# Moving the small PSUM copies of an attention stage from ScalarE to VectorE

## The reference

```python
for l in range(DEPTH):
    h = rms_norm(x, attn_norm[l])
    proj = h @ w_in[l]
    ...
    o_mla = mla_attention(...)      # softmax(q k^T * scale, causal) @ v, 8 heads
    o_nsa = nsa_attention(...)      # gates * (compressed, selected, window), 8 heads
    x = x + jnp.concatenate([o_mla, o_nsa], axis=-1) @ w_out[l]
    h = rms_norm(x, ffn_norm[l])
    x = x + conv_ffn(h, ...)
return rms_norm(x, final_norm)
```

## Time and profile before

| | |
|---|---|
| median of three runs | 1314.37 us |
| the profiled execution, its own time | 1314.45 us |
| its span in the profile | 1312.5 us |
| TensorE matmuls busy | 1272.6 us (97%) |
| VectorE busy | 687.2 us (52%) |
| ScalarE busy | 655.7 us (50%) |
| GpSimd busy | 67.8 us (5%) |
| attention stage of layer 0, of layer 1 | about 102 to 250 us, 749 to 897 us |

### The profile page before, as it was taken

One profiled execution on the slowest core, in us unless ns is written; L12 is line 12 of the kernel. 1 busy time (PEld: TensorE's weight loads), 2 busy tenths in 40 slices (PEclk: granted clock), 3 DMA queues, 4 the chain that ended last, 5 costly groups with the idle time before them and its releaser, 6 DMA issues.

```text
span 1312.5 us, 18515 instructions
## 1 busy us (share of the span) xinstructions
PE 1272.6 (97%) x6630; PEld 1050.4 (80%) x6630; DVE 687.2 (52%) x1194; ACT 655.7 (50%) x1223; POOL 67.8 (5%) x157
## 2 busy tenths in 40 slices
PE   8999999999999999999999999999999999999997
PEld 6997677788888888888889867677888888888886
DVE  5435667355555555533363456772655555554334
ACT  4337789445444444322352468892454544443223
POOL 2013110000000000000010311100000000000000
PEclk9999999999999999999999999999999999999999
DMA  6420101123333333322143210012223333333211
GB/s 205 124 89 1 65 1 46 35 80 105 98 98 98 98 97 100 108 96 97 53 121 94 65 65 1 1 50 84 81 76 96 97 96 97 98 103 118 96 64 64
DMA packets 121003, 107.04 MB, mean 82 GB/s; under 512 B 3764, under 2 KB 110486, under 8 KB 120947
## 3 DMA queue, kind: packets, MB, share of 16 engines
q1 hardware_dynamic: 118912, 101.13, 25.0%
q0 software_dynamic: 1456, 3.52, 0.9%
q10 hardware_dynamic: 578, 1.64, 0.3%
HBM read 104.19 MB, written 2.10 MB: 81 GB/s over the span
## 4 chain that ended last, share of the span: by engine, by line
PE 87%; DVE 7%; ACT 4%; issue 2%; DMA 0%; DVEq 0%
PE ps L1461 24%; PE ps L1463 24%; PE ps L1462 24%; PE ps L1648 3%; PE ps L1695 3%; PE ps L1629 2%; DVE probs L1210 1%; PE ps L1635 1%; PE ps L1634 1%; ACT probs L874 1%; DVE probs L1083 1%; DVE w_lo L581 1%; DVE x L1101 1%; PE ps L1662 1%; PE ps L1707 1%
## 5 line engine op out<-in xcount | busy, mean ns | idle before, releaser
L1461 PE MATMUL ps<-ht_hi,w_hi 128*128 128x512 f32 (+2 forms) x776 | 297.2, 383 | 2.5 <-DVE w_lo L581 2.5
L1463 PE MATMUL ps<-ht_hi,w_lo 128*128 128x512 f32 (+2 forms) x776 | 295.9, 381 | 0.0
L1462 PE MATMUL ps<-ht_lo,w_hi 128*128 128x512 f32 (+2 forms) x776 | 295.8, 381 | 0.0
L581 DVE TENSOR_TENSOR w_lo<-raw,w_hi 128x1024 fp32r<-128x1024 f32 (+4 forms) x196 | 218.6, 1140 | 96.3 <-ACT w_hi L574 86.2
L574 ACT ACTIVATE w_hi<-raw 128x1024 fp32r<-128x1024 f32 (+4 forms) x196 | 187.1, 983 | 94.1 <-PE ps L1463 93.9
L1377 DVE SCALAR_TENSOR_TENSOR conv<-ps,cols,conv 128x510 f32<-128x510 f32 (+1 forms) x176 | 127.6, 745 | 179.9 <-ACT conv L995 174.0
L1461 PEld LDWEIGHTS ps<-ht_hi,w_hi 128*128 128x128 f32 x776 | 145.8, 188 | 30.9 <-DVE w_lo L581 2.9
L1462 PEld LDWEIGHTS ps<-ht_lo,w_hi 128*128 128x128 f32 x776 | 145.9, 188 | 28.2 <-issue 0.5
L1463 PEld LDWEIGHTS ps<-ht_hi,w_lo 128*128 128x128 f32 x776 | 145.8, 188 | 27.7
L1461 PE MATMUL ps<-w_hi,ht_hi 128*128 128x430 f32 (+1 forms) x392 | 147.7, 377 | 3.3 <-DVE ht_lo L1090 2.5
L995 ACT ACTIVATE conv<-ps,cols 128x512 f32<-128x512 f32 x88 | 68.1, 774 | 160.0 <-PE ps L1463 159.7
(11 more groups left out here) (199 smaller groups left out, 1531.5 us busy)
## 6 DMA issues: line engine op xcount, KB each, us to landing
raw<-in_ffn_w_up_dram SPq DMA_DIRECT2D x88, 512.0 KB, 4.4
raw<-in_ffn_w_down_dram SPq DMA_DIRECT2D x44, 512.0 KB, 3.3
raw<-in_w_in_dram SPq DMA_DIRECT2D x32, 430.0 KB, 4.5
raw<-in_w_out_dram SPq DMA_DIRECT2D x16, 512.0 KB, 3.7
raw<-in_nsa_cmp_w_dram SPq DMA_DIRECT2D x8, 512.0 KB, 3.7
x<-in_x_dram ACTq DMA_DIRECT2D x3, 512.0 KB, 7.9
raw<-in_mla_w_uq_dram SPq DMA_DIRECT2D x4, 384.0 KB, 3.0
out_dram<-x SPq DMA_DIRECT2D x3, 512.0 KB, 2.6
```

The costliest lines, as they stand in the source:

```text
L581: last = nc.vector.tensor_tensor(d(w_lo)[:, :, d0:d1], r(raw)[:, :, r0:r1], d(w_hi)[:, :, d0:d1].bitcast(F32), ALU.subtract)
L1461: mm(o, lhs[0], rhs[0], start=start, stop=False)
L1462: mm(o, lhs[0], rhs[1], start=False, stop=False)
L1463: return mm(o, lhs[1], rhs[0], start=False, stop=stop)
```

## The change

The copy of a small unit's transposed probabilities is done by VectorE, in a new `copy_turn`, ahead of `row_max` in the same step in which ScalarE did it. ScalarE keeps the two copies of a big unit. `pt_act` and `pt_second` now count big units only, a new semaphore `pt_dve` counts small ones, and TensorE waits for the one that belongs to the unit. The copies have the same source, target and shape as before.

```diff
@@ semaphore counts
-    ... "pt_act": U, "pt_second": U // 2,
+    ... "pt_act": U // 2, "pt_dve": U // 2, "pt_second": U // 2,
@@
-        def pt_second_count(u):
-
-            return 2 * (u // T) + u % T + 1
+        def pt_count(u):
+
+            return 2 * (u // T) + u % 2 + 1
@@ ScalarE, evac_turn: the branch for small units goes
-                    else:
-                        activate(pt_half(u)[:, :, 0:blocks, q:q + P],
-                                 ps[:, bank, 0:2 * blocks * P].rearrange("p (a b q) -> p a b q", a=2, q=P), ACT.Copy)\
-                            .then_inc(pt_act, 1)
@@ ScalarE, the step
-                    if 0 <= s - T_LAG < U:
+                    if 0 <= s - T_LAG < U and big(s - T_LAG):
                         evac_turn(s - T_LAG)
@@ VectorE
+                def copy_turn(u):
+
+                    blocks, q = unit(u)[0] + 1, unit(u)[0] % 2 * P
+                    dve.wait_ge(t_done, at(t_done, l, turns(u, 0)))
+                    if u >= T:
+                        dve.wait_ge(pv_done, at(pv_done, l, u // 2 - 1))
+                    v.tensor_copy(pt_half(u)[:, :, 0:blocks, q:q + P],
+                                  ps[:, TURN_BANK[u, 0][0], 0:2 * blocks * P].rearrange("p (a b q) -> p a b q", a=2, q=P))\
+                        .then_inc(pt_dve, 1)
@@ VectorE, the step
+                    if 0 <= s - T_LAG < U and not big(s - T_LAG):
+                        copy_turn(s - T_LAG)
                     if s < U:
                         row_max(s)
@@ TensorE, turn_read
-                    if use is not None and use[1] == 0:
-                        pe.wait_ge(pt_act, at(pt_act, l, use[0] + 1))
+                    if use is not None and not big(use[0]):
+                        pe.wait_ge(pt_dve, at(pt_dve, l, pt_count(use[0])))
                     elif use is not None:
-                        pe.wait_ge(pt_second, at(pt_second, l, pt_second_count(use[0])))
+                        done = [pt_act, pt_second][use[1]]
+                        pe.wait_ge(done, at(done, l, pt_count(use[0])))
@@ TensorE, values
-                    pe.wait_ge(pt_act, at(pt_act, l, u + 1))
                     if big(u):
-                        pe.wait_ge(pt_second, at(pt_second, l, pt_second_count(u)))
+                        pe.wait_ge(pt_act, at(pt_act, l, pt_count(u)))
+                        pe.wait_ge(pt_second, at(pt_second, l, pt_count(u)))
+                    else:
+                        pe.wait_ge(pt_dve, at(pt_dve, l, pt_count(u)))
```

More of the change, by code:

```diff
@@ L156 @@
     "v_acc": T, "v_ready": T, "qk_acc": 3 * H // 2, "q_ready": H, "k_ready": H // 2, "kpe_done": 1,
-    "sc_done": 2 * U, "max_done": 2 * U, "exp_done": 2 * U, "t_done": 6 * NG, "pt_act": U, "pt_second": U // 2,
+    "sc_done": 2 * U, "max_done": 2 * U, "exp_done": 2 * U, "t_done": 6 * NG, "pt_act": U // 2, "pt_dve": U // 2, "pt_second": U // 2,
     "fac_ready": NG, "fac_done": NG, "fac_out": NG, "on_done": NG, "cmp_done": H // 2, "cmp_read": H // 2, "sum_done": H // 2, "pv_done": U // 2,
@@ L390, in hybrid_layers @@
         pt_act = sem("pt_act")
+        pt_dve = sem("pt_dve")
         pt_second = sem("pt_second")
@@ L882, in evac_turn @@
                         act.wait_ge(pv_done, at(pv_done, l, u // 2 - 1))
[L883 to L890, removed]
-                    else:
-                        activate(pt_half(u)[:, :, 0:blocks, q:q + P],
-                                 ps[:, bank, 0:2 * blocks * P].rearrange("p (a b q) -> p a b q", a=2, q=P), ACT.Copy)\
-                            .then_inc(pt_act, 1)
+                    activate(pt_half(u)[:, 0, 0:blocks, q:q + P],
+                             ps[:, TURN_BANK[u, 0][0], 0:blocks * P].rearrange("p (b q) -> p b q", q=P), ACT.Copy)\
+                        .then_inc(pt_act, 1)
+                    act.wait_ge(t_done, at(t_done, l, turns(u, 1)))
+                    activate(pt_half(u)[:, 1, 0:blocks, q:q + P],
+                             ps[:, TURN_BANK[u, 1][0], 0:blocks * P].rearrange("p (b q) -> p b q", q=P), ACT.Copy)\
+                        .then_inc(pt_second, 1)
                 def evac_factors(g):
```

## The result

The kernel after takes 1324.73 us, the median of seven runs (1321.32 to 1327.29); the kernel before, in seven runs beside it, 1315.98 (1314.37 to 1317.34). The ratio is 1.0069 with a 95% interval of 1.0059 to 1.0079: slower by 9.1 us (7.8 to 10.4). I had said slower, by 6.2. The sign and the place of the loss are right, the size is too small by a third, and the time lies 0.2 us above the range.

A forecast was written before the change was run, and what follows sets the result against it. The prediction took TensorE to set the pace, held through ScalarE by VectorE's bunched work before row maxima. Its step terms summed to 3.1 us a layer, 6.2 in two, on 1314.45: 1320.7 us, range 1316.5 to 1324.5.

The forecast's parts named there:

- What bounds the kernel: Attention stage: TensorE sets the pace; at its costly waits ScalarE itself came out of waiting for VectorE's row maxima.
- Rival A: ScalarE's backlog holds TensorE, so all waits on its copies (L892) go, 2.4 us a layer: 1309.6 us; chance 0.09.
- The price of a copy: On VectorE 415 ns for 256 columns, 684 for 512; a queue of ready work delayed by 0.95 us a group.
- Rival B: Copies as cheap as from SBUF, 0.57 for 0.95 us a group: 1317.4 us, or 1316.6 with more room; chance 0.12.
- The estimate of 1.06 a group: Group delay with 125 ns per VectorE access to PSUM and the measured slope; the sum would end 0.9 us later.
- The places: The step-by-step terms for one layer's attention stage: by how much TensorE ends later at each, summing to 3.1 us.
- gain of step 7: Steps 6 and 7: TensorE's 0.88 us wait for ScalarE's copy of unit 3 goes and stays gained, -0.88 a layer.
- steps 33 to 36: The 0.95 us fits in VectorE's idle gap of 1.59 us: 0, with bounds 0 and 0.95.
- rival C: More groups pay, copies cost 1.10, or step 7's gain fails: 1321 to 1323 each, 1325.8 together; beyond 1324.5 chance 0.11.
- Steps 25 to 28: Attention stage: the large copy meets the row maximum when both are just ready, +0.05 us a layer.
- the delay runs to the end: After the stage TensorE goes into the output projection with weights ready, so the 6.2 us of two layers stays.
- The 1320.7: Forecast time in us: 1314.45, the profiled execution, plus 6.2, 0.5% slower; the forecast's chance 0.68.

The follow-up runs named there:

- before_late: Kernel before, all small copies left on ScalarE, with VectorE's `out_lo` of the NSA pairs and four weight splits one step later: 1313.50 us, -2.5 against before.
- after_cast: Kernel after, with GpSimd's second pair of casts made to wait for the transposes of unit 23: 1322.89 us, +8.3 us against the kernel before.

## Why the prediction was right, and where it was wrong

**What bounds the kernel: right.** The waits named ScalarE, and what held them was VectorE's row maxima. `before_late` is the test that leaves the copies alone: 2.5 us gained by order on VectorE only. Rival A is refuted; ScalarE's relief turned into waits for `nmax`.

**The price of a copy: right.** 415 and 684 ns foretold, 418 and 686 measured; a group pays 0.92 to 0.94 where I had 0.95. Rival B, copies as cheap as from SBUF, falls. The estimate of 1.06 a group from the 125 ns per access on the Trainium skill's page "Perfetto Trace Analysis" (section Optimizing Scalar/DVE Operations) is 0.12 above what the groups paid.

**The places: nine of eleven within 0.1 us.** The gain of step 7 was 0.78, not 0.88; beyond 0.1 lie steps 33 to 36, which cost 0.12, not 0, and the term below. The first two are part of rival C, in small.

**Two steps failed.** The one whose term was mis-sized reads "Steps 25 to 28: the large copy meets the row maximum when both are just ready: +0.05". The term measured 0.41. I looked at when TensorE's transposes and scores were ready, and not at what VectorE did before: its `factors` there overlaps GpSimd's casts and, once it starts behind the second of them, takes twice as long. In the kernel before that could be seen in layer 1 (1.56 us at 836.11), where an idle time of 0.25 behind it hid it; in layer 0 `factors` was ahead of that cast (0.72 at 188.85). The small copy put it behind, and the large copy used up the idle time. `after_cast` takes back 0.32 of it.

**The other, and the larger one, is the clock,** which the prediction put at nothing without a reason: its sum treated a wait as its own length ("the delay runs to the end"). In the kernel after, the two standstills at the end of each stage brought a stretch at half clock behind them, 3.0 us of the profiled execution and about 1.3 us of the mean over runs. That the mean is due to the longer standstills is argued, not shown: the falls all stand behind a standstill, and eight of eleven behind a lengthened one, but no run adds a standstill by itself, and three falls stand where the change does nothing. What decides whether one brings a fall stays open.

**The base was too low as well.** The 1320.7 is 6.2 on top of 1314.45, a single execution, at mean clock 0.998. The kernel before takes 1315.98 in the median of the seven runs beside the kernel after. Of the 4.0 us between 1320.7 and 1324.73, 1.5 are this base; on 1315.98 the same sum gives 1322.2.

Foretold 6.2; queues 7.3, of which 0.7 for the casts, 0.2 for step 7 and 0.2 for steps 33 to 36; clock some 1.3; some 0.5 left, within the interval.

## What to carry to other kernels

Before work is moved off the engine that a wait names, follow that engine back: if it came out of a wait itself, the queue to shorten is the one behind, and reordering there can gain what moving work would lose. A copy pays on another engine only at the place where that engine's timeline is idle when the data is ready; of the 24 units a layer, unit 3 was one here, and the only one that I moved by itself. When a copy is priced into a gap, read the gap in each layer, and look at GpSimd too: an idle time that hides a rare stretch is not free.

## What the hardware showed that I had not expected

A TensorE standstill costs more than its length at times. With waits of 1.21 and 0.71 us close together (busy 1.47, 0.87 and 1.52 of three times 2 us) the granted clock fell to 0.50, and 128x512 matmuls took 0.63 us for 0.39, for about 1.5 us of added time. Not every such standstill does it, and the same kernel at the same place in the other layer may pass.

A VectorE tensor_tensor with both inputs in SBUF took 1.47 us beside GpSimd's casts and 0.69 without them; a PSUM copy of the same width beside the same casts was not lengthened at all. Which side pays went by which started first: a third of a microsecond earlier, the same tensor_tensor took 0.72 and GpSimd's two casts 2.48 for 2.11. A copy of 0.34 us ahead of it was enough to turn this round.
